# SSD stage of a hybrid decoder step: the chunk state updated ahead of skip and gate, and the memory stages' first rows loaded a stage earlier

## The chip, the cores and the metric

One core of one Trainium2 chip runs the whole program. The metric is device time in microseconds (us) of one execution; lower is better. The kernel before was timed three times: 4456.8 us median, 4452.07 to 4466.3.

## What is computed

One inference step of a decoder trunk for a prompt of 1024 tokens and 8 sample tokens, all in float32. What matters here:

- The input projection gives, besides the attention's q, k and v, the columns z, xBC and dt of a Mamba-2 state-space layer (SSD). xBC goes through a causal convolution over 4 tokens and SiLU. The prompt is scanned in 8 chunks of 128 tokens: within a chunk `y_diag = (C B^T * decay) (x dt)`; from the state carried in, `y_off = C state * exp(cs)`; then `state = chunk_decay * state + B^T (x dt decay_to_end)`.
- The chunk's output is `y = (y_diag + y_off + D x) * SiLU(z)` and then RMS normalised. The sum of the first two terms is called `y`, `D x` is the skip, `SiLU(z)` the gate.
- The 8 sample tokens take one recurrent step of the same layer from a stored state.
- `x += concat(rmsnorm(attention), rmsnorm(ssd)) @ w_out`, then `x +=` cross-attention into 256 memory tokens, then `x +=` an expert layer with 128 retrieved experts per token, then a final norm.

## The kernel before, in words

The program is a chain of stages, each a block of five instruction streams (PE, ACT, DVE, POOL, SP) with semaphores of its own; a barrier of all engines ends each (`Stage.__exit__`). The order is: attention of the prompt, attention of the samples, `ssd_prompt`, `ssd_sample_inputs`, `memory_kv_and_sample_step`, `memory_read`, `memory_read_sample`, `expert_mix`. The last one takes about two thirds of the time. Within a stage each engine runs its instructions in the written order, and a wait holds up all that stands behind it on its engine.

**`ssd_prompt`** works in turns. In turn (t, u = t + 1) the engines finish chunk t ("back") and prepare chunk u ("front"). PE: `tokens(t)` (transposes `xs0`, `xs1` at L1054, the B and C products `bc`, and `yo0`, `yo1`, which multiply C by the state, L1093), decays G0 (L1101), the four projections x0, x1, x2, dt of chunk u (L1062), decays G1, transposes of xBC, the scan, projection z0, the state products `grown` (L1130), projection z1, `summed`. DVE: `tokens`, `scaled` (writes the rows of chunk t - 1), `begin_y`, `middle(u)` (evacuates x0 and x2, L1383), `decays`, half of the convolution taps (L995, L999), `rates`, `finish(t)` (L1425), `summed(u)`. ACT: `tokens(t)` (copies `xs0`, `xs1` out of PSUM, L1195), `middle`, `decays`, `channels`, `convolved`, `gated(t)` (L1243: waits for `y_gated`, squares `y`), `gates(u)` (L1249: SiLU(z) into `zs`), `summed(u)` (exponentials). POOL does the skip `xskip`, the other half of the taps and the norm's factor.

PSUM banks are shared by name in a fixed order (`back_fills`): bank 4 is used by `xs0`, `yo1` and `yd1`, bank 5 by `xs1`, G0, G2 and `st0`, bank 6 by `bc`, G1, G3 and `st1`, bank 7 by `yo0` and `yd0`. A fill waits until the engine that reads the bank's last content has freed it. `st0` and `st1` are the two halves of the chunk's state products, `yd0` and `yd1` those of `y_diag`. `finish(t)` holds the edit: it adds `yd0` and `yd1` to `y` (L1429), adds the skip (L1432), multiplies by the gate (L1434), signals `y_gated`, and then multiplies the state (L1438), adds `st0` and `st1` (L1443) and signals `state_ready`, for which PE's `yo0` of the next chunk waits.

**`memory_kv_and_sample_step`** does two things at once. PE and ACT turn the 256 memory tokens into keys `mk` and values `mv` (`w_mk`, `w_mv`), and PE transposes the keys for DVE to copy into `mkT`. DVE makes the samples' recurrent step over the 4 MB state, which lies in the buffer of `w_out`. SP loads all inputs, stores the new state, then loads the first half of `w_out` (L1689), stores the step's result `y_pairs` (L1692), loads the second half of `w_out` (L1693), loads the result back in another layout as `y` (L1695), stores `mk` and `mv`, and stores the normalised `y` as the samples' rows of the scratch tensor `mixed` (L1701). `y` goes through DVE (skip, gate, L1799 and L1801), ACT (square, L1759), POOL (factor) and DVE (scale, L1808).

**`memory_read`** takes the first two tiles of 128 prompt tokens (`READ = 2`) through `w_out`, the norm and the cross-attention. SP loads `mixed` rows, `x`, the gain of the next norm, `w_mq`, `w_mo`; PE transposes the rows (`turn_mixed`, L1914), DVE multiplies by the gain (`mixed_rows`, L2084; it first waits for `gain_in`, L2150), and PE starts the residual (L1931). PE's priming signals (L1999 to L2002) come ahead of the first transposes; SP's first load waits for one of them.

**`memory_read_sample`** does the same for the 8 sample tokens; it loads their `mixed` rows (L2211) and `x` (L2212), and PE starts with transposes (L2240).

Of the kernel before, what the change touches and what calls it, by code (L numbers as in the profile page):

```python
# [32 lines left out]
P = 128  # L33
# [873 lines left out]
def ssd_prompt(nc, io, psum, shared, w_zx):  # L907
# [7 lines left out]
    with Stage(nc) as stage:  # L915
# [428 lines left out]
        def _(dve):  # L1344
# [80 lines left out]
            def finish(t):  # L1425
# [4 lines left out]
                dve.drain()  # L1430
                dve.wait_ge(xskip_ready.sem, xskip_ready.this(t))
                nc.vector.tensor_tensor(y[:], y[:], xskip[:], ALU.add)  # L1432
                dve.drain()
                nc.vector.tensor_tensor(y[:], y[:], zs[:], ALU.mult)  # L1434
                dve.drain()
                dve.sem_inc(y_gated.sem, 1)

# [7 lines left out]
                dve.sem_inc(state_ready.sem, 1)  # L1445

# [183 lines left out]
def memory_kv_and_sample_step(nc, io, psum, shared, mkT, mv, w_out, w_mo, w_out_in):  # L1630
# [9 lines left out]
    with Stage(nc) as stage:  # L1640
# [26 lines left out]
        def _(sp):  # L1667
# [14 lines left out]
            sp.dma_start(w_mv[:], io["w_mv"].rearrange("(b p) n -> p b n", p=P)).then_inc(wv_in, 16)  # L1682
            sp.wait_ge(state_ready, 1)
# [50 lines left out]
        def _(act):  # L1734
# [36 lines left out]
        def _(dve):  # L1771
# [29 lines left out]
            nc.vector.tensor_tensor(y[:], y[:], gates[:], ALU.mult).then_inc(gated, 1)  # L1801
            for m in range(MT):
# [4 lines left out]
            dve.wait_ge(yrstd_ready, 1)  # L1807
            nc.vector.tensor_scalar(y[:], y[:], yrstd[:], None, ALU.mult).then_inc(out_ready, 1)  # L1808
# [1651 lines left out]
```

## Time and profile before

| what | value |
|---|---|
| median of the runs | 4456.8 us (4452.07 to 4466.3) |
| the profiled execution's own time | 4453.82 us |
| its span, first to last instruction | 4452.0 us |
| mean granted TensorE clock | 0.939 |
| PE busy | 3833.0 us (86%) |
| DVE busy | 2495.7 us (56%) |
| ACT busy | 1309.2 us (29%) |
| POOL busy | 1356.9 us (30%) |

The page gives busy times by engine, then by groups of instructions (line, engine, operation, tile). Times in a timeline are microseconds from the span's start. "PEld" is PE's weight load, "SPq" and "DVEq" the sequencers of SP and DVE. The text in brackets at the end of a row is how long the engine had been idle, and what released it. The granted clock is given as a share of full speed: 1.00 is 2.4 GHz, 0.50 is 1.2 GHz. The SSD stage of the prompt lies at about 490 to 1028 us, the samples' inputs until 1074, the memory keys until 1168, the read until 1343, the sample read until about 1500 and the experts after it.

### The profile page before, as it was taken

Reading aid. Unit: us, or ns where it says so; the run is one execution under the profiler, and the core shown is the slowest. Engines: PE = TensorE matmul, PEld = TensorE weight load, DVE = VectorE, ACT = ScalarE, POOL = GpSimd, SP = SyncE. Lnnn points to the kernel's source line nnn. Section 1 sums busy time; section 2 is a strip of 40 time slices with the busy share of each in tenths; the row PEclk is TensorE's granted clock in tenths of the full one; section 3 lists DMA queues with packets and bytes.
Section 4 is the critical chain, followed back from the end, with each engine's and each line's share of the span. In section 5 each row is a group of like instructions: output and inputs, shape, how many; then the busy total and the mean of one; then the engine's idle time right before and its main releaser. Section 6 shows DMA issues by size and latency. Waiting matters only on the chain.

```text
span 4452.0 us, 41910 instructions
## 1 busy us (share of the span) xinstructions
PE 3833.0 (86%) x11597; PEld 1973.0 (44%) x11597; DVE 2495.7 (56%) x5472; ACT 1309.2 (29%) x3879; POOL 1356.9 (30%) x1243
## 2 busy tenths in 40 slices
PE   8998789887788799998889999889999888877876
PEld 4555254552362445543445554345554344433332
DVE  2333255663312477654577754587755468766664
ACT  2333032331011133342233342323324233333332
POOL 0000033330000133443433434433344343333442
PEclk9996799998897899999999999999999999999999
DMA  6001000004604599999999999999999999999997
GB/s 211 29 28 39 28 15 19 19 9 142 245 10 166 208 418 418 419 418 421 420 403 405 418 420 420 421 399 406 411 420 414 421 419 402 418 418 397 419 420 297
DMA packets 227230, 1316.62 MB, mean 296 GB/s; under 512 B 27224, under 2 KB 43517, under 8 KB 93344
## 3 DMA queue, kind: packets, MB, share of 16 engines
q0 software_dynamic: 148608, 1082.20, 58.8%
q1 hardware_dynamic: 77272, 232.15, 13.9%
q8 instruction: 79, 1.29, 0.1%
q14 instruction: 119, 0.97, 0.1%
q10 hardware_dynamic: 1152, 0.00, 0.0%
HBM read 1283.65 MB, written 32.68 MB: 296 GB/s over the span
## 4 chain that ended last, share of the span: by engine, by line
DMA 27%; PE 25%; DVE 8%; issue 3%; ACT 3%; DVEq 1%; ACTq 0%; POOL 0%; POOLq 0%
DMA ex_ring<-in_expert_uv,ex_idx 26%; PE psum L2752 16%; DVE ex_ring L3137 4%; PE psum L2781 4%; PE psum L2730 3%; ACT ex_diag L2933 1%; PE psum L2800 1%; ACT ex_weight L2928 0%; PE psum L2825 0%; DMA ex_ring<-in_expert_uv,ex_idxT 0%; PE psum L2842 0%; POOL ex_ring L2672 0%; DMA pair_p<-scratch_mixed 0%; DVE ex_best_at L3063 0%; ACT ex_dots L2924 0%
## 5 line engine op out<-in xcount | busy, mean ns | idle before, releaser
L2752 PE MATMUL psum<-ex_ring,ex_diag 128*128 128x512 f32 x4096 | 1920.2, 613 | 332.4 <-ACT ex_diag L2933 308.4
L3137 DVE CUSTOM_DVE_ANT_0 ex_ring<-ex_ring,ex_x_rows 128x1024 f32<-128x1024 f32 x1024 | 1250.5, 1226 | 827.6 <-DMA ex_ring<-in_expert_uv,ex_idx 755.6
L2672 POOL DMA_INDIRECT ex_ring<-in_expert_uv,ex_idx x1024 | 1139.8, 1113 | 1751.4 <-PE psum L2752 1544.1
L2752 PEld LDWEIGHTS psum<-ex_ring,ex_diag 128*128 128x128 f32 x4096 | 771.7, 195 | 1304.9 <-issue 851.6
L2924 ACT ACTIVATE ex_dots<-ex_dots 128x2 f32<-128x2 f32 x512 | 104.1, 203 | 1792.1 <-DVEq L3140 1791.6
L2933 ACT ACTIVATE ex_diag<-ident,ex_weight 128x128 f32<-128x128 f32 x1024 | 355.0, 393 | 36.9 <-issue 1.7
L1062 PE MATMUL psum<-w_zx,ssd_hT 128*128 128x512 f32 (+1 forms) x768 | 294.2, 539 | 21.8 <-DMA ssd_hT<-scratch_hT 21.1
L2730 PE MATMUL psum<-ex_xT,ex_chunk 128*128 128x256 f32 (+1 forms) x1280 | 277.9, 361 | 4.2 <-ACT ex_sub L2909 2.9
L2730 PEld LDWEIGHTS psum<-ex_xT,ex_chunk 128*128 128x128 f32 x1280 | 230.2, 192 | 98.3 <-issue 77.3
L2928 ACT ACTIVATE ex_weight<-ex_gates,ex_dots 128x1 f32<-128x1 f32 x1024 | 245.7, 287 | 36.2 <-issue 1.1
L1062 PEld LDWEIGHTS psum<-w_zx,ssd_hT 128*128 128x128 f32 x768 | 136.9, 192 | 175.1 <-issue 153.1
L320 PE MATMUL psum<-w_qkv,att_hT 128*128 128x512 f32 x384 | 186.6, 633 | 10.6 <-DMA w_qkv<-in_w_in 4.3
L2781 PE MATMUL psum<-ex_chunk,pair_turned_rows 128*128 128x512 f32 x384 | 180.5, 592 | 0.0
L320 PEld LDWEIGHTS psum<-w_qkv,att_hT 128*128 128x128 f32 x384 | 73.5, 201 | 101.4 <-issue 94.1
L615 DVE TENSOR_TENSOR att_turned<-psum,bias 128x512 f32<-128x512 f32 (+1 forms) x64 | 41.8, 658 | 99.8 <-PE psum L347 98.8
L2781 PEld LDWEIGHTS psum<-ex_chunk,pair_turned_rows 128*128 128x128 f32 x384 | 71.1, 190 | 59.9 <-issue 57.4
L536 POOL TENSOR_TENSOR att_ms<-att_ms,att_part 128x1 f32<-128x1 f32 x8 | 1.5, 189 | 303.3 <-ACTq L446 303.3
L2800 PE MATMUL psum<-pair_turned_rows,ex_chunk 128*128 128x256 f32 x384 | 90.7, 379 | 0.0
L2842 PE MATMUL psum<-ex_chunk,pair_turned_rows 128*128 128x512 f32 x192 | 90.2, 592 | 0.0
L1383 DVE TENSOR_SCALAR ssd_xbc<-psum,ssd_rstd 128x512 f32<-128x512 f32 x16 | 12.0, 750 | 131.0 <-PE psum L1062 131.0
L2800 PEld LDWEIGHTS psum<-pair_turned_rows,ex_chunk 128*128 128x128 f32 x384 | 72.8, 190 | 28.2 <-issue 20.6
L3137 DVE DVE_READ_ACCUMULATOR2_ANT ex_dots<- 128x1 f32 x1024 | 83.8, 82 | 0.0
(455 smaller groups left out, 3707.6 us busy)
## 6 DMA issues: line engine op xcount, KB each, us to landing
ex_chunk<-in_route_wq SPq DMA_DIRECT2D x80, 512.0 KB, 7.9
ex_chunk<-in_w_out SPq DMA_DIRECT2D x48, 512.0 KB, 9.1
ex_ring<-in_expert_uv,ex_idx POOLq DMA_INDIRECT x1024, 20.5
ex_chunk<-in_read_wq SPq DMA_DIRECT2D x24, 512.0 KB, 8.0
ex_chunk<-in_w_mo SPq DMA_DIRECT2D x24, 512.0 KB, 7.9
w_zx<-in_w_in SPq DMA_DIRECT2D x1, 10304.0 KB, 35.8
w_out<-in_w_out SPq DMA_DIRECT2D x2, 4096.0 KB
w_out<-in_cache_mem_k SPq DMA_DIRECT2D x8, 1024.0 KB, 13.5
```

What stands on the lines that cost most here:

```text
L320: ins = nc.tensor.matmul(out[:], hT[:, b, :], w_qkv[:, b, c * BANK:(c + 1) * BANK], start=(b == 0), stop=(b == DB - 1))
L1062: ins = nc.tensor.matmul(out[:, 0:n], hT[:, b, :], w_zx[:, b, col:col + n], start=(b == 0), stop=(b == DB - 1))
L2672: nc.gpsimd.indirect_dma_start(out=ring[:, n % RING, :], out_offset=None, in_=io["expert_uv"], in_offset=bass.IndirectOffsetOnAxis(ap=idx[ ...
L2730: ins = nc.tensor.matmul(psum[6 + k % 2][:, 0:n], w[:, b, :], xT[:, b, 0:n], start=(b == 0), stop=(b == DB - 1))
L2752: ins = nc.tensor.matmul(psum[c][:], diag[:, q % 3, s, :], ring[:, n % RING, D + c * BANK:D + (c + 1) * BANK], start=(n % SLOTS == 0), sto ...
L2781: ins = nc.tensor.matmul(psum[2 + 2 * a + c][:], mT[:, b, a * P:(a + 1) * P], w[:, c * BANK:(c + 1) * BANK], start=(b == 0), stop=(b == 2 ...
L2800: ins = nc.tensor.matmul(psum[2 + d % 4][:, 0:N], w[:, b, :], hT[:, b, :], start=(b == 0), stop=(b == DB - 1), skip_group_check=True)
L2842: ins = nc.tensor.matmul(psum[2 + 2 * a + c][:], oT[:, b, a * P:(a + 1) * P], w[:, c * BANK:(c + 1) * BANK], start=(b == 0), stop=(b == DB ...
L2924: nc.scalar.activation(dots[:, q % 8, :], dots[:, q % 8, :], ACT.Gelu)
L2928: nc.scalar.activation(weight[:, q % 2, s:s + 1], gates[:, g % 2, a, at:at + 1], ACT.Copy, scale=dots[:, q % 8, s:s + 1])
L2933: ins = nc.scalar.activation(diag[:, q % 3, s, :], ident[:], ACT.Copy, scale=weight[:, q % 2, s:s + 1])
L3137: nc.vector.tensor_tensor_reduce(ring[:, n % RING, 0:D], ring[:, n % RING, 0:D], x_rows[:, tile % 3, :], 1.0, 0.0, ALU.mult, ALU.add, dots ...
```

## The change

In `finish`, the state update is put ahead of skip and gate:

```diff
                     nc.vector.tensor_tensor(y[:, cols], y[:, cols], src[:], ALU.add).then_inc(free, 1)
-                dve.drain()
-                dve.wait_ge(xskip_ready.sem, xskip_ready.this(t))
-                nc.vector.tensor_tensor(y[:], y[:], xskip[:], ALU.add)
-                dve.drain()
-                nc.vector.tensor_tensor(y[:], y[:], zs[:], ALU.mult)
-                dve.drain()
-                dve.sem_inc(y_gated.sem, 1)
-
                 nc.vector.tensor_tensor(by_head(state[:]), by_head(state[:]), per_head(esums[:, 1, :]), ALU.mult)
...
                 dve.drain()
                 dve.sem_inc(state_ready.sem, 1)
+                dve.wait_ge(xskip_ready.sem, xskip_ready.this(t))
+                nc.vector.tensor_tensor(y[:], y[:], xskip[:], ALU.add)
+                dve.drain()
+                nc.vector.tensor_tensor(y[:], y[:], zs[:], ALU.mult)
+                dve.drain()
+                dve.sem_inc(y_gated.sem, 1)
```

In `memory_kv_and_sample_step`, SP loads the first 128 rows of `mixed` and the samples' `x` behind `w_mv`; `y` is loaded ahead of the second half of `w_out`, and stored ahead of `mv`; ACT squares `y` ahead of the second tile of `mv`; DVE scales `y` ahead of the copies into `mkT`:

```diff
             sp.dma_start(w_mv[:], io["w_mv"].rearrange("(b p) n -> p b n", p=P)).then_inc(wv_in, 16)
+            sp.dma_start(mixed_rows[:], io["mixed"][0:P, :]).then_inc(rows_in, 16)
+            sp.dma_start(own_x[:], io["x_sample"]).then_inc(own_in, 16)
...
-            sp.dma_start(w_out[:, DB:2 * DB, :], w_out_rows[:, DB:2 * DB, :]).then_inc(w_out_in, 16)
             sp.wait_ge(pairs_stored, 16)
             sp.dma_start(y[:], io["rows3"]).then_inc(y_in, 16)
+            sp.dma_start(w_out[:, DB:2 * DB, :], w_out_rows[:, DB:2 * DB, :]).then_inc(w_out_in, 16)
             sp.wait_ge(k_ready, MT)
             sp.dma_start(io["p_mem_k"].rearrange("(m p) n -> p m n", p=P), mk[:]).then_inc(stored, 16)
+            sp.wait_ge(out_ready, 1)
+            sp.dma_start(io["mixed"][SEQ:TOKENS, D:2 * D], y[:]).then_inc(out_stored, 16)
             sp.wait_ge(v_ready, MT)
             sp.dma_start(io["p_mem_v"].rearrange("(m p) n -> p m n", p=P), mv[:]).then_inc(stored, 16)
-            sp.wait_ge(out_ready, 1)
-            sp.dma_start(io["mixed"][SEQ:TOKENS, D:2 * D], y[:]).then_inc(out_stored, 16)
...
             for m in range(MT):
+                if m == 1:
+                    act.wait_ge(gated, 1)
+                    nc.scalar.activation(junk[0:DEC, :], y[:], ACT.Square, accum_out=yms[:]).then_inc(yms_ready, 1)
                 act.wait_ge(projected, 4 + 2 * m + 2)
...
-            act.wait_ge(gated, 1)
-            nc.scalar.activation(junk[0:DEC, :], y[:], ACT.Square, accum_out=yms[:]).then_inc(yms_ready, 1)
...
             nc.vector.tensor_tensor(y[:], y[:], gates[:], ALU.mult).then_inc(gated, 1)
+            dve.wait_ge(yrstd_ready, 1)
+            nc.vector.tensor_scalar(y[:], y[:], yrstd[:], None, ALU.mult).then_inc(out_ready, 1)
             for m in range(MT):
...
             dve.drain()
-            dve.wait_ge(yrstd_ready, 1)
-            nc.vector.tensor_scalar(y[:], y[:], yrstd[:], None, ALU.mult).then_inc(out_ready, 1)
```

In `memory_read`, the buffer `mixed` is now the one filled a stage before. SP's order is `x`, `w_mq`, second `mixed` rows, `w_mo`, gain, second `x`; once the second turn's rows have been transposed, it loads the samples' `mixed` rows into the same buffer. DVE's wait for the gain moves to its first use:

```diff
-            load_mixed(0)
             load_x(0)
-            sp.dma_start(gain_ffn[:], io["norm_ffn_w"].broadcast_to([P, D])).then_inc(gain_in, 16)
             sp.dma_start(w_mq[:], io["w_mq"].rearrange("(b p) n -> p b n", p=P)).then_inc(w_mq_in, 16)
+            sp.sem_inc(mixed_in.sem, 16)
             load_mixed(1)
             sp.dma_start(w_mo[:], io["w_mo"].rearrange("(b p) n -> p b n", p=P)).then_inc(w_mo_in, 16)
+            sp.dma_start(gain_ffn[:], io["norm_ffn_w"].broadcast_to([P, D])).then_inc(gain_in, 16)
             load_x(1)
+            sp.wait_ge(mixed_turned.sem, mixed_turned.last(READ))
+            sp.dma_start(mixed[0:DEC, :], io["mixed"][SEQ:TOKENS, :]).then_inc(own_in, 16)
...
             def turn_mixed(u):
-                pe.wait_ge(mixed_in.sem, mixed_in.this(u))
+                if u:
+                    pe.wait_ge(mixed_in.sem, mixed_in.this(u))
+                else:
+                    pe.wait_ge(rows_in, 16)
...
             def ffn_rows(t):
 
+                if t == 0:
+                    dve.wait_ge(gain_in, 16)
...
-            dve.wait_ge(gain_in, 16)
             mixed_rows(0)
```

In `memory_read_sample`, the loads of the rows and of `x` go; `x` lies in `x1`, to which the projection is added:

```diff
-            sp.dma_start(mixed[:], io["mixed"][SEQ:TOKENS, :]).then_inc(loaded, 16)
-            sp.dma_start(x[:], io["x_sample"]).then_inc(loaded, 16)
...
-            pe.wait_ge(loaded, 32)
+            pe.wait_ge(own_in, 32)
...
-            dve.wait_ge(loaded, 32)
+            dve.wait_ge(own_in, 32)
...
-                ins = nc.vector.tensor_tensor(x1[:, cols], psum[1 + c][0:DEC, :], x[:, cols], ALU.add)
+                ins = nc.vector.tensor_tensor(x1[:, cols], psum[1 + c][0:DEC, :], x1[:, cols], ALU.add)
```

The buffer `mixed` and the semaphores `rows_in` and `own_in` are made in `program`, ahead of the memory stages.

## Rows read from the trace of the kernel before

**Rows 1.** Waits, 560 to 1040 us: waiter <- releaser: us in all, times, longest.

```profile
PE psum L1054 <- DVE ssd_state L1443: 22.3, 7, 3.9
...
PEld psum L1093 <- ACT ssd_xs L1185: 8.9, 8, 1.3
```

**Rows 2.** Timeline, end of one chunk: start, duration, engine, line, operation, [idle before <- releaser].

```profile
744.54 1.28 DVE L1429 TENSOR_TENSOR ssd_y<-ssd_y,psum 128x512 f32<-128x512 f32 x2 [0.19 <-issue]
...
745.92 1.23 DVE L1432 TENSOR_TENSOR ssd_y<-ssd_y,ssd_xskip 128x1024 f32<-128x1024 f32 x1
...
748.50 1.06 ACT L1245 ACTIVATE ssd_junk<-ssd_y 128x1024 f32<-128x1024 f32 x1 [3.15 <-DVEq L1435]
...
749.86 1.28 DVE L1443 TENSOR_TENSOR ssd_state<-ssd_state,psum 128x512 f32<-128x512 f32 x2
...
750.60 1.11 PE L1054 MATMUL psum<-ident,ssd_cv 128*128 128x128 f32 x4 [2.34 <-DVE ssd_state L1443]
...
753.70 1.08 ACT L1185 ACTIVATE ssd_xs<-psum 128x512 f32<-128x512 f32 x2 [0.98 <-issue]
...
756.66 1.15 PE L1101 MATMUL psum<-tri,ssd_decay 128*128 128x128 f32 x8 [0.24 <-issue]
```

**Rows 3.** Timeline, DVE in the middle of the same chunk.

```profile
717.38 0.75 DVE L1383 TENSOR_SCALAR ssd_xbc<-psum,ssd_rstd 128x512 f32<-128x512 f32 x1 [12.98 <-PE psum L1062]
...
724.12 2.04 DVE L995 TENSOR_TENSOR ssd_cv<-ssd_xbcT,conv 128x768 f32<-128x768 f32 x1
```

**Rows 4.** Windows: stretch, length, busy us of PE, PEld, DVE, ACT, POOL, granted clock, DMA.

```profile
754.00:756.00 2.00, 2.00 (x3) 0.50 (x2) 1.15 (x1) 0.79 (x2) 1.10 (x1) 0.50 0.03 0
```

**Rows 5.** Timeline, the end of the next chunk.

```profile
809.58 1.06 ACT L1245 ACTIVATE ssd_junk<-ssd_y 128x1024 f32<-128x1024 f32 x1 [3.15 <-DVEq L1435]
...
815.44 1.12 PE L1093 MATMUL psum<-ssd_state,ssd_cv 128*128 128x512 f32 x2 [0.24 <-ACT ssd_xs L1185]
...
816.80 1.15 PE L1101 MATMUL psum<-tri,ssd_decay 128*128 128x128 f32 x8 [0.24 <-issue]
```

**Rows 6.** Timeline, the last chunk's end.

```profile
1015.16 3.75 PE L1130 MATMUL psum<-ssd_xend,ssd_bm 128*128 128x512 f32 x4 [0.38 <-issue]
...
1018.37 1.06 ACT L1245 ACTIVATE ssd_junk<-ssd_y 128x1024 f32<-128x1024 f32 x1 [6.39 <-DVEq L1435]
```

**Rows 7.** Timeline, the tail of memory_kv_and_sample_step.

```profile
1148.98 0.28 SPq L1695 DMA_DIRECT2D step_y<-scratch_rows  x1
...
1149.74 0.47 SPq L1699 DMA_DIRECT2D out_p_mem_v<-mv  x1
1159.40 1.21 DVE L1799 TENSOR_TENSOR step_y<-step_y,step_xs 8x1024 f32<-8x1024 f32 x1 [16.51 <-DMA step_y<-scratch_rows]
...
1165.14 0.30 SPq L1701 DMA_DIRECT2D scratch_mixed<-step_y  x1
```

**Rows 8.** DMA issues, 1060 to 1550 us: line, queue, count, KB, us to landing.

```profile
out_p_mem_v<-mv SPq DMA_DIRECT2D x1, 1024.0 KB, 14.8
```

**Rows 9.** Timeline, the start of memory_read_sample.

```profile
1343.49 0.30 SPq L2211 DMA_DIRECT2D rs_mixed<-scratch_mixed  x1
...
1346.90 1.87 PE L2240 MATMUL psum<-ident,rs_mixed 8*128 8x8 f32 x16 [12.32 <-DMA rs_x<-in_x_sample]
```

**Rows 10.** Timeline, the start of memory_read.

```profile
1169.34 0.36 SPq L1872 DMA_DIRECT2D read_mixed<-scratch_mixed  x1
...
1174.22 1.97 PE L1914 MATMUL psum<-ident,read_mixed 128*128 128x128 f32 x8 [24.57 <-DMA read_mixed<-scratch_mixed]
...
1178.34 1.97 PE L1914 MATMUL psum<-ident,read_mixed 128*128 128x128 f32 x8 [2.16 <-DVE read_mT L2084]
...
1181.23 30.34 PE L1931 MATMUL psum<-w_out,read_mT 128*128 128x512 f32 x64 [0.92 <-DVEq L2091]
```

**Rows 11.** Windows around PE's transposes of the memory tokens (L1712).

```profile
1080.80:1084.37 3.57, 3.56 (x16) 3.27 (x16) 2.07 (x3) 3.41 (x5) 0.89 (x2) 0.53 1.01 403
1084.37:1087.78 3.41, 0.00 (x1) 0.00 (x0) 0.69 (x1) 0.16 (x1) 0.00 (x0) 0.97 1.03 419
```

More of the change, by code:

```diff
@@ L1627, in _, with memory_kv_and_sample_step @@
             nc.vector.tensor_tensor(dt[:], raw[:], neg[:], ALU.add).then_inc(dt_ready, 1)
-def memory_kv_and_sample_step(nc, io, psum, shared, mkT, mv, w_out, w_mo, w_out_in):
+def memory_kv_and_sample_step(nc, io, psum, shared, mkT, mv, w_out, w_mo, own_x, mixed_rows, w_out_in, rows_in, own_in):
     ident, gain = shared["ident"], shared["gain_mem"]
@@ L1806, in _, with memory_read @@
             dve.drain()
-            dve.wait_ge(yrstd_ready, 1)
-            nc.vector.tensor_scalar(y[:], y[:], yrstd[:], None, ALU.mult).then_inc(out_ready, 1)
-def memory_read(nc, io, psum, shared, w_out, w_mq, w_mo, mkT, mv, w_out_in):
+def memory_read(nc, io, psum, shared, w_out, w_mq, w_mo, mkT, mv, mixed, w_out_in, rows_in, own_in):
     ident = shared["ident"]
@@ L1820, in memory_read @@
         sb, sem, event = stage.buffer, stage.semaphore, stage.event
-        mixed = sb("read_mixed", [P, 2 * D])
         x = sb("read_x", [P, D])
@@ L2154, in _, with memory_read_sample @@
             ffn_rows(READ - 1)
-def memory_read_sample(nc, io, psum, shared, w_out, w_mq, w_mo, x1):
+def memory_read_sample(nc, io, psum, shared, w_out, w_mq, w_mo, x1, mixed, own_in):
     ident = shared["ident"]
@@ L2166, in memory_read_sample @@
         sb, sem = stage.buffer, stage.semaphore
-        mixed, x, junk, q = sb("rs_mixed", [DEC, 2 * D]), sb("rs_x", [DEC, D]), sb("rs_junk", [DEC, D]), sb("rs_q", [DEC, D])
+        junk, q = sb("rs_junk", [DEC, D]), sb("rs_q", [DEC, D])
         mT, hT = sb("rs_mT", [P, 2 * DB, DEC]), sb("rs_hT", [P, DB, DEC])
@@ L2185, in memory_read_sample @@
         v = [places[b % VP] for b in range(DEC)]
-        loaded, turned, mT_ready, summed, x1_ready = (sem("rs_" + n) for n in ("loaded", "turned", "mT_ready", "summed", "x1_ready"))
+        turned, mT_ready, summed, x1_ready = (sem("rs_" + n) for n in ("turned", "mT_ready", "summed", "x1_ready"))
         x1_turned, hT_ready, ms_ready, rstd_ready, projected, q_ready = (
@@ L3398, in program @@
             ssd_sample_inputs(nc, io, psum, shared, w_zx)
-        w_out_in = nc.alloc_semaphore("w_out_in")
+        w_out_in, rows_in, own_in = (nc.alloc_semaphore(n) for n in ("w_out_in", "mixed_rows_in", "own_rows_in"))
         mkT, mv = sb("mkT", [P, DB, N_MEM]), sb("mv", [P, N_MEM // P, D])
@@ L3405, in program @@
             w_mo = memory.enter_context(nc.sbuf_tensor("w_mo", [P, DB, D], F32))
-            memory_kv_and_sample_step(nc, io, psum, shared, mkT, mv, w_out, w_mo, w_out_in)
+            mixed = memory.enter_context(nc.sbuf_tensor("read_mixed", [P, 2 * D], F32))
+            memory_kv_and_sample_step(nc, io, psum, shared, mkT, mv, w_out, w_mo, x1, mixed, w_out_in, rows_in, own_in)
             w_mq = memory.enter_context(nc.sbuf_tensor("w_mq", [P, DB, D], F32))
-            memory_read(nc, io, psum, shared, w_out, w_mq, w_mo, mkT, mv, w_out_in)
-            memory_read_sample(nc, io, psum, shared, w_out, w_mq, w_mo, x1)
+            memory_read(nc, io, psum, shared, w_out, w_mq, w_mo, mkT, mv, mixed, w_out_in, rows_in, own_in)
+            memory_read_sample(nc, io, psum, shared, w_out, w_mq, w_mo, x1, mixed[0:DEC, :], own_in)
         expert_mix(nc, io, psum, shared, mkT, mv)
```

## The prediction

> **What bounds the kernel now.** I read four views: the waits over the SSD stage, the timeline of one chunk's end, the timeline of the memory stages, and the DMA issues. The long expert stage after them is not edited and begins behind a barrier, so what the early stages gain or lose arrives at the end unchanged.
>
> In the waits, PE has one wait that the first edit aims at: its transposes at L1054 (`xs1`, whose PSUM bank the state update frees) stand 22.3 us in all, seven times, for the state adds at L1443. Below it stands a smaller one: the matmuls of `yo1` at L1093 wait for ACT's copy of `xs0` (L1185) [rows 1]. The timeline shows both in one chunk end [rows 2]. DVE adds `y` until 745.82, adds the skip at 745.92, gates, and ACT squares at 748.50; the state adds end at 749.86 + 1.28 = 751.14, and PE resumes at 750.60, in the middle of them. But PE does not run on freely: ACT copies `xs0` only at 753.70, and the decays of L1101 (G0), which precede the next projection, start at 756.66. In the code ACT is strictly ordered: convolved, gated (waits `y_gated`), gates, summed, then the next chunk's tokens. From `y_gated` to the `xs` copies ACT needs 753.70 - 748.50 = 5.2 us. `yo1` shares bank 4 with `xs0`, G0 shares bank 5 with `xs1`, so both need those copies.
>
> Is that a closed loop? DVE's evacuation of `x2` waits 12.98 us for PE's projection, and its taps begin at 724.12 and run until the finish at 744.54 [rows 3, 2]. So PE's projections lead to DVE's taps, to the finish, to `y_gated`, to ACT's copies, and back to PE. A delay of `y_gated` delays the whole chunk.
>
> **SSD: the moved state update.** Removed is one drain; moved are the state multiply, its drain, two adds and their drain, from behind `y_gated` to ahead of it. Before, the state part ends 751.14 - 748.50 = 2.64 us after `y_gated` [rows 2]. With the saved drain (about 0.1, the gap 745.82 to 745.92) and the overlap of two signals I take 2.5 us per chunk by which `y_gated` is later; ends 2.4 and 2.6. `xskip` and the state fills are long there (the `grown` matmuls precede projection z1), so nothing new is waited for. What is queued behind the wait on ACT: square, two gates, the exponentials and the `xs` copies, hence PE's `yo1`, G0 and DVE's `xdt`.
>
> PE's own gain is real but goes nowhere: `xs1`, `bc` and `yo0`, which now run from 750.60 to about 754 at the slow clock, would start 2.6 us sooner and be done near 751. PE would then wait for ACT until 753.70 + 0.55 (one of the two copies) + 2.5, about 756.8: one idle stretch of nearly 6 us in place of 2.34.
>
> The clock is the second price. At this boundary the granted clock is 0.50, the 1.2 GHz level, at 754 to 756 [rows 4], and from ACT's square to G0 pass 756.66 - 748.50 = 8.16 us. At another boundary PE is nearer the 2.4 GHz level and it is 816.80 - 809.58 = 7.22 us; there `yo1` takes 1.12 us and is plainly released by ACT [rows 5]. The seven lie between, so about 0.5 us per chunk is paid already. After an idle of 6 us I expect PE to restart at the low level, so that `yo1`, G0 and the first projections run slowly. Here, after an idle of 2.34 us, the low level went on from PE's restart at 750.60 to about G0 at 756.66, 6.1 us [rows 2]. Half of that, 3.0, is the most that I charge, less the 0.5 already paid; with a little for slower drains, +2.9. The other end is -0.5, if PE comes back at full clock. I take +1.7, nearer the high end, because the nearest row is a shorter idle that already cost clock.
>
> Seven boundaries: 7 x (2.5 + 1.7) = 29.4 us. The eighth finish has no next chunk. There PE's state matmuls run from 1015.16 to 1018.91 and ACT squares at 1018.37 [rows 6]; afterwards the second state add waits for 1018.91, ends near 1019.6, and skip and gate (2.6) bring `y_gated` to about 1022.3: +3.9, which the scaled rows, the state copies into `y` and the last store follow. SSD together +33.3, ends 7 x (2.4 - 0.5) + 3.5 = +16.8 and 7 x (2.6 + 2.9) + 4.5 = +43.
>
> **Memory keys and sample step.** The 1 MB of first mixed rows and the 32 KB of `x_sample` go onto SP's queue behind `w_mv`, ahead of the state's store; SP stands idle there waiting for DVE, and the queue drains before that store. Cost 0; if the cover were gone, 1 MB. At the tail, `y`'s load is issued at 1148.98 and used at 1159.40, held up behind the second half of `w_out`; its result is stored at 1165.14 [rows 7]. With the load ahead of that half, `y` is there about 3 us after issue, some 7 us earlier, and ACT's square (now ahead of the second `mv` copy), DVE's scaling (now ahead of four mkT copies) and the out store follow. But the same bytes still go: 4 MB of `w_out` now start only after 1149.3, when the queue has run dry, and the stores of `mem_k` and `mem_v` come behind. `mem_v` was issued at 1149.74 and landed 14.8 us later, 1164.5 [rows 7, 8]; a dry queue costs up to the 3.4 us that the sample's loads need from issue to use (1346.90 less 1343.49, [rows 9]), which puts `mem_v` at 1167 to 1168, about where the stage ended. Also the added waits: ACT's wait for `gated` holds back the second `mv` copy and so the `mem_v` store; it and SP's `out_ready` wait end near 1157, ahead of the queue's drain. I take 0, ends -2.5 and +2.5.
>
> **Memory read.** PE's first transposes start at 1174.22 on a load issued at 1169.34, the second pair at 1178.34, and the residual at 1181.23 [rows 10]. Afterwards the rows are there, and DVE no longer waits for the gain. SP's first load had to wait for PE's priming, so PE can start near 1169.4; first pair 1.97 and from the second pair to the residual 1181.23 - 1178.34 = 2.89, with a tenth between: residual at 1174.4, 6.8 us earlier; I take 6.6, ends 5.0 and 9.5. `w_mq` and `w_mo` are needed only after the residual's 30.34 us; the gain load, moved behind `w_mo`, is hidden by the whole first tile. The new SP wait for the second turn holds only the store of `x2`, much later.
>
> Would the clock rise sooner? In the stage before, 16 transposes (3.56 us) at 0.53 were followed by 0.97 [rows 11]: transposes alone did bring the clock up, so part of the high end 9.5 is real. The Trainium skill says otherwise: "TensorE: Matmul & The Clock Gate", Part 4, has transposes not counting as busy; by it this stage gives 6.6 and no more, while the row allows up to the whole 9.5. The trace disagrees with that sentence. I keep 6.6, since here the transposes come in two pairs with a gap.
>
> **Sample read.** The two loads go; PE starts at the barrier, near SP's first load, 1343.49, and a signal, in place of 1346.90 [rows 9]: -3.2, ends -2.5 and -3.5.
>
> **Sum.** +33.3 + 0 - 6.6 - 3.2 = +23.5 us. The profiled execution's own time is 4453.8, so 4477.3; the median of the runs shown is 3.0 higher, so 4480. Ends: +16.8 - 15.5 = +1.3 and +43 - 5 = +38, or 4458 and 4495. A difference of 0.3%, 13.4 us, is about what a measurement of this kernel can tell.
>
> **Rivals.** *PE's wait is the bound (faster).* If the state update is what PE's chunk waits for, 22.3 us go, the last finish costs 3.9, the memory stages give 9.8: 4456.8 - 28.2, about 4429. It decides if ACT's `xs` copies would not be late, that is if `y_gated` had more than 2.5 us of slack. For it: it is PE's largest wait in the stage. Against: ACT's square itself starts 0.05 us after DVE's gate ends, and PE is released by ACT [rows 1, 5]. 6%. The Trainium skill, "Perfetto Trace Analysis", Optimization Strategy, has one look for the gaps of the bound engine and make what blocks them start sooner; read on the largest gap alone, it gives this rival. The trace shows the next blocker right behind.
> *The clock costs nothing more (same).* 17.5 + 3.9 in SSD, memory at its best -12: +9.4, 4466, within 0.3%. For it: the present idle already lowers the clock at several boundaries. 17%.
> *The clock stays low longer (slower still).* +43 - 5: 4495. 12%.
> My forecast has 65%. The range 4460 to 4494 holds it, most of the second rival and much of the third. Faster 0.08 (the first rival and a little of the second's tail), same 0.16, slower 0.76.
>
> **What would show it.** Right: PE's wait on L1443 gone; the wait of L1093 on ACT's `xs` grown to about 6 us, seven times; chunk period about 4 us longer; the granted clock low at G0; ACT's square about 2.5 us later after the adds; residual about 6 us after SP's first load of the read stage instead of 12; sample PE at its stage's start. Wrong: a chunk period unchanged or shorter, or `yo1` released by something other than ACT.

## The result, and the profile after

| | before | after |
|---|---|---|
| median of 7 runs, us | 4455.2 (4448.4 to 4466.3) | 4478.0 (4474.9 to 4481.9) |
| profiled span, us | 4452.0 | 4473.1 |
| mean granted clock | 0.939 | 0.940 |

The ratio is 1.0048, interval 1.0039 to 1.0057: slower by 17 to 25 us. The forecast was 4480.

Where the 21.1 us of the two spans lie is read from the timelines, from the start of one stage's first operation to that of the next:

| stretch | before, us | after, us | difference | predicted |
|---|---|---|---|---|
| start to G0 of the first SSD chunk | 574.27 | 571.93 | -2.3 | not edited |
| SSD, to the sample inputs' first load | 454.35 | 486.53 | +32.2 | +33.3 |
| sample inputs | 45.86 | 45.08 | -0.8 | not edited |
| memory keys and sample step | 94.86 | 96.86 | +2.0 | 0 |
| memory read | 174.15 | 167.26 | -6.9 | -6.6 |
| sample read, to the experts' first load (before: at 1485.2) | 141.73 | 140.45 | -1.3 | -3.2 |
| expert stage to the end | 2966.8 | 2965.0 | -1.8 | not edited |

The unedited stretches differ by up to 2.3 us; a difference of that size in one row is not evidence of anything.

**SSD.** The waits of the changed kernel over 560 to 1070 us (waiter <- releaser: us in all, times, longest):

```profile
ACT ssd_junk L1245 <- DVEq L1442: 49.8, 8, 10.1
PEld psum L1093 <- ACT ssd_xs L1185: 48.2, 8, 6.9
PE psum L1093 <- ACT ssd_xs L1185: 36.2, 7, 5.3
...
PE psum L1054 <- DVE ssd_state L1435: 7.0, 7, 1.2
```

The wait that the edit aimed at fell from 22.3 us to 7.0 [rows 1]. A new one of 36.2 us stands in its place: `yo1` on ACT's copy of `xs0`. (The 8.9 us of [rows 1] are of the weight loads, PEld; their row is now 48.2.) The sum of PE's waits rose. The timeline of the same chunk end shows why (start, duration, engine, line, operation, idle before and releaser):

```profile
750.71 1.28 DVE L1429 TENSOR_TENSOR ssd_y<-ssd_y,psum 128x512 f32<-128x512 f32 x2 [0.19 <-issue]
751.91 1.22 DVE L1430 TENSOR_TENSOR ssd_state<-ssd_state,ssd_esums 128x1024 f32<-128x1024 f32 x1
...
753.20 1.29 DVE L1435 TENSOR_TENSOR ssd_state<-ssd_state,psum 128x512 f32<-128x512 f32 x2
...
753.94 0.80 PE L1054 MATMUL psum<-ident,ssd_cv 128*128 128x128 f32 x4 [0.97 <-DVE ssd_state L1435]
...
757.21 1.06 ACT L1245 ACTIVATE ssd_junk<-ssd_y 128x1024 f32<-128x1024 f32 x1 [5.69 <-DVEq L1442]
...
762.41 1.08 ACT L1185 ACTIVATE ssd_xs<-psum 128x512 f32<-128x512 f32 x2 [0.98 <-issue]
...
763.06 2.07 PE L1093 MATMUL psum<-ssd_state,ssd_cv 128*128 128x512 f32 x2 [5.27 <-ACT ssd_xs L1185]
...
765.37 2.07 PE L1101 MATMUL psum<-tri,ssd_decay 128*128 128x128 f32 x8 [0.24 <-issue]
```

From the start of DVE's `y` adds to ACT's square it is 757.21 - 750.71 = 6.50 us, where it was 748.50 - 744.54 = 3.96 [rows 2]: 2.54 later. ACT's own 5.2 us from the square to the `xs` copies did not change (762.41 - 757.21). PE resumed its transposes 1 us after it stopped in place of 2.34, ran `yo0`, and then stood 5.27 us in front of `yo1`.

The windows of the same stretch (length, busy us of PE, PEld, DVE, ACT, POOL, granted clock, DMA) show the second price:

```profile
757.00:763.00 6.00, 0.79 (x1) 0.00 (x0) 0.51 (x3) 4.62 (x9) 0.98 (x3) 0.78 0.00 0
763.00:765.00 2.00, 1.94 (x2) 0.50 (x2) 1.24 (x2) 0.49 (x2) 1.40 (x1) 0.50 0.03 0
765.00:767.00 2.00, 1.76 (x8) 1.64 (x8) 2.00 (x3) 0.00 (x0) 1.54 (x1) 0.50 0.00 0
767.00:769.00 2.00, 2.00 (x7) 1.06 (x6) 1.51 (x3) 0.00 (x0) 0.00 (x0) 0.76 0.00 0
769.00:771.00 2.00, 2.00 (x6) 0.85 (x5) 1.16 (x2) 0.00 (x0) 0.00 (x0) 1.00 0.65 262
```

After the idle of 5.27 us PE comes back at 0.50, the 1.2 GHz level, and the clock is at 1.00 again only about 5 us later, within 767 to 769. The idle is not where it first fell: `yo0` already ran at 0.50 (754.4 to 757.7), then the clock stood at 1.00 while PE was idle (757.8 to 761.1) and was at 0.50 again from 761.2, ahead of `yo1`. `yo1` takes 2.07 us where the next chunk end of before had 1.12, and G0 takes 2.07 where it took 1.15 [rows 5].

ACT's eight squares start at 627.32, 692.31, and so on to 1016.67 and 1048.35; before, at 627.13, 687.56, to 990.87 and 1018.37. The six periods between the first seven are 389.35 us, 64.89 each, against 363.74, 60.62 each: +4.27, where the prediction had 2.5 + 1.7 = 4.2. The last finish:

```profile
1041.47 3.43 PE L1130 MATMUL psum<-ssd_xend,ssd_bm 128*128 128x512 f32 x4 [0.38 <-issue]
...
1044.94 0.69 DVE L1435 TENSOR_TENSOR ssd_state<-ssd_state,psum 128x512 f32<-128x512 f32 x1 [0.70 <-PE psum L1130]
...
1048.35 1.06 ACT L1245 ACTIVATE ssd_junk<-ssd_y 128x1024 f32<-128x1024 f32 x1 [10.06 <-DVEq L1442]
```

The second state add waits for PE's state matmuls, as predicted. From their start to the square it is 6.88 us; it was 3.21 [rows 6]: +3.7, predicted +3.9.

**Keys stage.** The timeline of its tail, and the start of the read stage:

```profile
1179.93 0.29 SPq L1694 DMA_DIRECT2D step_y<-scratch_rows  x1
1180.27 0.38 SPq L1695 DMA_DIRECT2D w_out<-in_w_out  x1
...
1181.79 1.21 DVE L1800 TENSOR_TENSOR step_y<-step_y,step_xs 8x1024 f32<-8x1024 f32 x1 [9.51 <-DMA step_y<-scratch_rows]
...
1187.23 0.31 SPq L1699 DMA_DIRECT2D scratch_mixed<-step_y  x1
1187.58 0.37 SPq L1701 DMA_DIRECT2D out_p_mem_v<-mv  x1
...
1200.40 0.36 SPq L1876 DMA_DIRECT2D read_x<-in_x_prompt  x1
1201.92 3.51 PE L1916 MATMUL psum<-ident,read_mixed 128*128 128x128 f32 x16 [23.82 <-issue]
1206.50 27.70 PE L1936 MATMUL psum<-w_out,read_mT 128*128 128x512 f32 x64 [1.07 <-DVEq L2096]
```

`y` is used 1.9 us after its load is issued, where that took 1159.40 - 1148.98 = 10.4 [rows 7]. The stage is no shorter, for it now ends on the store of `mem_v`. The DMA issues give it (line, queue, count, KB, us to landing):

```profile
out_p_mem_v<-mv SPq DMA_DIRECT2D x1, 1024.0 KB, 11.5
```

Issued at 1187.58, it lands at 1199.1, and the read stage's first load goes out at 1200.40. The store has 4 MB of `w_out` and 1 MB of `mem_k` ahead of it; both were issued only once `rows3` had made its round trip, and in that time the queue ran dry:

```profile
1178.50:1181.50 3.00, 0.00 (x0) 0.00 (x0) 0.00 (x0) 0.00 (x0) 0.00 (x0) 0.91 0.38 109
```

That is a window of 3 us in which the DMA engines moved 109 GB/s; the windows of 3 us on both sides moved 410 and 317. Whether this gap costs the stage its 2.0 us is settled with `fed_queue`, at the end of the experiments: it does not.

**Memory read.** The residual starts 1206.50 - 1200.40 = 6.1 us after the stage's first load, where it was 1181.23 - 1169.34 = 11.9 [rows 10]: 5.8 sooner. It also takes 27.70 us in place of 30.34. The windows of its start, of the changed kernel:

```profile
1201.90:1205.40 3.50, 3.47 (x16) 2.82 (x16) 1.76 (x3) 0.00 (x0) 0.00 (x0) 0.57 0.96 348
1205.40:1206.50 1.10, 0.03 (x1) 0.03 (x1) 0.91 (x2) 0.00 (x0) 0.00 (x0) 1.00 0.98 372
```

All 16 transposes now run in one piece, and the clock stands at 1.00 before the first matmul of the residual. Before, the residual began at 0.50:

```profile
1181.20:1185.00 3.80, 3.77 (x5) 1.73 (x6) 0.00 (x0) 0.00 (x0) 0.00 (x0) 0.50 1.02 413
1185.00:1187.00 2.00, 2.00 (x4) 0.73 (x4) 0.00 (x0) 0.00 (x0) 0.00 (x0) 0.62 1.05 418
```

The 0.62 of the second window puts the rise at 1186.5, so the first 5.3 us of the residual ran at half speed, which is the 2.6 us of its length. So 5.8 + 2.6 = 8.4 us are gained by the residual's end, and the rest of the stage gives 1.5 back.

**Sample read.** PE starts with the stage:

```profile
1367.66 0.30 SPq L2217 DMA_DIRECT2D rs_gain_ffn<-in_norm_ffn_w  x1
1367.71 1.84 PE L2244 MATMUL psum<-ident,read_mixed 8*128 8x8 f32 x16 [9.03 <-PEq L127]
```

That is 0.05 us after SP's first load in place of 3.41 [rows 9], a gain of 3.4. At the stage's end 1.3 of it is left: the loads of `k` come 2.9 us sooner, but DVE then waits 15.8 us for the next projection, where it waited 14.1. That projection takes longer:

```profile
1402.79 15.60 PE L2250 MATMUL psum<-w_mq,rs_hT 128*8 128x512 f32 x32 [0.32 <-DVE rs_hT L2338]
```

Before, it took 13.90 us, all at 1.00. Here the granted clock was 0.50 from 1402.86 to 1406.20, and once more in this stage from 1484.8 to 1488.1. Of the kernels below, which all have this stage, `mem_only`, `both` and `filler` take 13.90 us for the projection and 138.2, 138.0 and 138.2 us for the stage: 3.5 to 3.8 less than before. `w_out_back` and `fed_queue` take 15.60, and 140.4 and 140.5 like this kernel. So the edit gains about 3.5 us here, and the two low stretches of this execution hid about 2 of them.

### The profile page after: what moved, and what is told of

Same layout as the page of the kernel before. It is cut to its first block, busy times and chain, and to the rows that moved or that the text cites. A ratio compares the mean times of both kernels' runs of the same rounds, so it can differ in the third digit from the quotient of the medians.

```text
span 4473.1 us, 41903 instructions
## 1 busy us (share of the span) xinstructions
PE 3836.9 (86%) x11597; PEld 1971.7 (44%) x11597; DVE 2495.2 (56%) x5472; ACT 1308.6 (29%) x3879; POOL 1365.8 (31%) x1243
## 4 chain that ended last, share of the span: by engine, by line
DMA 27%; PE 24%; DVE 7%; issue 3%; ACT 3%; DVEq 1%; ACTq 0%; POOL 0%; POOLq 0%
DMA ex_ring<-in_expert_uv,ex_idx 26%; PE psum L2756 16%; DVE ex_ring L3141 4%; PE psum L2785 3%; PE psum L2734 3%; ACT ex_diag L2937 1%; PE psum L2804 1%; ACT ex_weight L2932 0%; PE psum L2829 0%; DMA ex_ring<-in_expert_uv,ex_idxT 0%; PE psum L2846 0%; POOL ex_ring L2676 0%; DMA pair_p<-scratch_mixed 0%; DVE ex_best_at L3067 0%; DVE ex_top_at L3036 0%
## 5 line engine op out<-in xcount | busy, mean ns | idle before, releaser
L2932 ACT ACTIVATE ex_weight<-ex_gates,ex_dots 128x1 f32<-128x1 f32 x1024 | 245.7, 287 | 36.2 <-issue 1.1
L1062 PEld LDWEIGHTS psum<-w_zx,ssd_hT 128*128 128x128 f32 x768 | 138.0, 193 | 175.4 <-issue 153.7
L320 PE MATMUL psum<-w_qkv,att_hT 128*128 128x512 f32 x384 | 187.9, 637 | 11.2 <-DMA w_qkv<-in_w_in 4.3
L320 PEld LDWEIGHTS psum<-w_qkv,att_hT 128*128 128x128 f32 x384 | 73.9, 202 | 102.5 <-issue 94.9
```

Source lines behind the costliest of these rows:

```text
L320: ins = nc.tensor.matmul(out[:], hT[:, b, :], w_qkv[:, b, c * BANK:(c + 1) * BANK], start=(b == 0), stop=(b == DB - 1))
L1062: ins = nc.tensor.matmul(out[:, 0:n], hT[:, b, :], w_zx[:, b, col:col + n], start=(b == 0), stop=(b == DB - 1))
L2932: nc.scalar.activation(weight[:, q % 2, s:s + 1], gates[:, g % 2, a, at:at + 1], ACT.Copy, scale=dots[:, q % 8, s:s + 1])
```

## The experiments

The theory: a chunk's start on PE is released by two signals that lie close together. One is the state adds (bank 5, hence `xs1`); the other is ACT's `xs` copies, which stand behind the gated `y` in ACT's order (banks 4 and 5, hence `yo1` and G0). The edit speeds the first and delays the second, and PE comes out of the longer idle at a low clock. The rival of that: the loss is in PE's or DVE's own work, or in the memory stages. Ratios below are each against the kernel before, timed beside it on the same chip (median 4457.7 for the first four, 4457.1 for the others).

**The two halves of the change alone.** `ssd_only` is the kernel before with the diff of `finish`, and nothing of the memory stages:

```diff
-                dve.drain()
-                dve.wait_ge(xskip_ready.sem, xskip_ready.this(t))
...
                 nc.vector.tensor_tensor(by_head(state[:]), by_head(state[:]), per_head(esums[:, 1, :]), ALU.mult)
...
                 dve.sem_inc(state_ready.sem, 1)
+                dve.wait_ge(xskip_ready.sem, xskip_ready.this(t))
+                nc.vector.tensor_tensor(y[:], y[:], xskip[:], ALU.add)
...
+                dve.sem_inc(y_gated.sem, 1)
```

> The kernel before with the state update ahead of skip and gate, and none of the memory edits. My theory: ACT's copies of xs, which wait for the gated y, close the loop; y is gated 2.5 us later in each of seven chunks, the lower clock after PE's longer idle adds about 1.7, and the last chunk's end 3 to 4: +32 us, 4487 (4480 to 4493). The rival, PE's wait for the state adds is the bound and 22.3 us of it go: about 4437.

Measured: 4489.2, ratio 1.0075 (1.0058 to 1.0092). From the first G0 to the sample inputs' first load it takes 1065.86 - 578.45 = 487.4 us against 454.35: +33.1, where the prediction's sum for SSD was +33.3. Its waits over 560 to 1070 us:

```profile
PE psum L1093 <- ACT ssd_xs L1185: 37.9, 7, 6.8
...
PE psum L1054 <- DVE ssd_state L1435: 7.1, 7, 1.1
```

`mem_only` is the changed kernel with the old `finish`:

```diff
+                dve.drain()
+                dve.wait_ge(xskip_ready.sem, xskip_ready.this(t))
+                nc.vector.tensor_tensor(y[:], y[:], xskip[:], ALU.add)
...
+                dve.sem_inc(y_gated.sem, 1)
                 nc.vector.tensor_tensor(by_head(state[:]), by_head(state[:]), per_head(esums[:, 1, :]), ALU.mult)
...
                 dve.sem_inc(state_ready.sem, 1)
-                dve.wait_ge(xskip_ready.sem, xskip_ready.this(t))
...
-                dve.sem_inc(y_gated.sem, 1)
```

> The kernel before with the memory edits and the old order in DVE's finish. My theory from the prediction: the keys stage unchanged, the read 6.6 us and the sample read 3.2 us shorter: -9.8, 4445. From the trace of the changed kernel: keys stage 2 us longer, read 6.9 and sample read 1.3 shorter: -6, 4449. The rival, that the slow time came from the memory stages: above 4460.

Measured: 4444.9, ratio 0.9974 (0.9963 to 0.9985). Its PE waits in SSD are those of before (22.4 us on the state adds; 8.9 of the weight loads on the copies). So the loss is all in SSD, and the memory edits are a gain of 7 to 16 us by themselves. The two halves sum to +31.5 - 12.8 = +18.7; the whole change measured +22.8 in its own runs.

**The other blocker alone, and both.** If ACT's `xs` copies are the second releaser, moving them ahead of `gated` takes that signal off the gated `y`. `act_only` does this to the kernel before, in ACT's `turn`:

```diff
                     load_rstd(u)
-                if back:
-                    tokens(t)
                 if front:
                     middle(u)
...
                     convolved(u)
+                    tokens(u)
                 if back:
                     gated(t)
```

> The kernel before, with ACT copying the next chunk's xs ahead of squaring the gated y, so that nothing of PE's chunk start waits for the gated y any more. If ACT's copies alone set the chunk before (so that the state adds were fully hidden): about 2.5 us a chunk go, 4437. If the two blockers were near a tie, as the timelines with yo1 only 0.24 us behind yo0 suggest: -0.2 to -1 a chunk, 4451 (4446 to 4456). If ACT's order has no part in it: 4455.

Measured: 4454.6, ratio 1.0002 (0.999 to 1.0013). The time excludes 4437, the case of ACT's copies alone, but it cannot tell a near tie (4451) from no part at all (4455). The trace tells more. ACT's copies no longer hold `yo1`, but PE still stands for the state adds; its waits over 560 to 1040 us:

```profile
PE psum L1054 <- DVE ssd_state L1442: 20.8, 7, 4.0
PEld psum L1093 <- issue: 6.9, 16, 0.5
```

A chunk takes (985.69 - 624.66) / 6 = 60.17 us, 0.45 less than before. `both` is the same edit in the changed kernel:

```diff
-                if back:
-                    tokens(t)
...
                     convolved(u)
+                    tokens(u)
                 if back:
                     gated(t)
```

> The changed kernel with ACT copying the next chunk's xs ahead of squaring the gated y. If the gated y blocks PE through ACT's order alone, the moved state update now pays: PE goes from xs0 to the projections without a long wait, about 7 us a chunk less than in the changed kernel (4.2 given back and some 3 of the old wait), 4428 (4418 to 4438), well below both kernels. If something else of the moved update made the chunk longer (DVE's order, the clock by itself), it stays above 4465.

Measured: 4425.2, ratio 0.9937 (0.9921 to 0.9954). A chunk takes (973.76 - 629.79) / 6 = 57.33 us, 7.6 less than in the changed kernel and 3.3 less than before. Its waits over 560 to 1030 us, and one chunk end:

```profile
PE psum L1062 <- ACT ssd_zs L1185: 5.2, 4, 1.6
...
PE psum L1054 <- DVE ssd_state L1434: 4.0, 4, 1.0
```

```profile
742.10 1.08 ACT L1185 ACTIVATE ssd_xs<-psum 128x512 f32<-128x512 f32 x2 [3.19 <-PE psum L1054]
...
744.60 1.06 ACT L1245 ACTIVATE ssd_junk<-ssd_y 128x1024 f32<-128x1024 f32 x1 [1.42 <-DVEq L1441]
...
745.12 1.15 PE L1101 MATMUL psum<-tri,ssd_decay 128*128 128x128 f32 x8 [0.24 <-issue]
...
747.30 15.29 PE L1062 MATMUL psum<-w_zx,ssd_hT 128*128 128x512 f32 x35 [1.03 <-ACT ssd_zs L1185]
```

```profile
744.00:748.00 4.00, 2.73 (x13) 1.48 (x12) 2.89 (x6) 3.15 (x5) 1.84 (x3) 1.00 0.00 0
```

At this end G0 starts 0.52 us after ACT's square instead of 8.16 (0.14 to 1.84 us at the seven ends), with the clock at 1.00, and the next blocker is a third one: the bank of `z1`, which ACT's gates free behind their wait for the gated `y`. The four kernels make a table:

| | state update behind the gate | state update first |
|---|---|---|
| ACT's copies behind `gated` | 4457.7 (before) | 4478.0 (after); 4489.2 without the memory edits |
| ACT's copies first | 4454.6 | 4425.2, with the memory edits |

Each edit alone gives nothing or a loss. Together, and with the memory edits' 12.8 us set aside, they give 4457.7 - 12.8 - 4425.2 = 19.7 us by the medians. No kernel with both edits and without the memory edits was run. The trace of `both` gives less: its SSD takes 439.3 us against 454.35, so 15.0.

**The clock.** `filler` adds matmuls to the changed kernel, one behind the transposes of `xs0` and four between `yo0` and `yo1`, into front bank 0. Their results are read by nobody; they only keep PE busy where it stood idle.

```diff
+                def fill_time(n):
+                    pe.wait_ge(front_fills.free[0], front_fills.at("x2", t + 1))
+                    for b in range(n):
+                        nc.tensor.matmul(psum[0][:], ident[:], w_zx[:, b, 0:BANK], start=True, stop=True)
...
                 for g in range(SSD_G):
+                    if g:
+                        fill_time(4)
                     out, full = begin(f"yo{g}", t)
```

> The changed kernel with five extra matmuls a chunk (one behind xs0, four between yo0 and yo1), whose results nobody reads, in the time in which PE waits for ACT. If the lower clock after that idle is a price of its own (G0 2.07 us in place of 1.15, the projections behind it 1.2 us longer): the granted clock stays up, -1.2 to -2 a chunk, 4468 (4463 to 4473). If the chunk is only later by the gated y: 4478.

Measured: 4471.9, ratio 1.0033 (1.0018 to 1.0047). The time is as expected, but the clock did not stay up as a whole: it held at the start of two of the six chunks only, and the mean chunk is 1.16 us shorter, just under the expected 1.2 to 2. The windows around G0 at one such chunk end, and at one where it fell:

```profile
768.00:770.00 2.00, 1.75 (x11) 1.29 (x11) 1.80 (x4) 0.00 (x0) 2.00 (x1) 1.00 0.00 0
...
704.00:705.00 1.00, 0.88 (x5) 0.88 (x6) 0.80 (x2) 0.00 (x0) 1.00 (x1) 0.66 0.00 0
705.00:707.00 2.00, 2.00 (x7) 1.48 (x7) 2.00 (x3) 0.00 (x0) 1.24 (x1) 0.50 0.00 0
```

The two chunks with the clock held take 823.92 - 761.25 = 62.67 and 1015.11 - 952.42 = 62.69 us; the other four 64.15 to 64.35; the changed kernel's 64.89. This prices the clock: 64.89 - 62.68 = 2.2 us per chunk. Without it the chunk is still 62.68 - 60.62 = 2.06 longer than before. That is the 2.54 of the later `y` less the half microsecond of clock that the kernel before already paid. PE's idle in front of `yo1` was 3.34 us at four of the six ends: at two of these the clock held, at two it fell within G0. At the other two ends it was 2.14 and 2.17 us, and the clock fell within `yo1`. So the length of that idle does not decide it; what does stays open.

**Half of the move.** `half` is the kernel before with the state multiply alone put ahead of skip and gate:

```diff
+                nc.vector.tensor_tensor(by_head(state[:]), by_head(state[:]), per_head(esums[:, 1, :]), ALU.mult)
                 dve.drain()
                 dve.wait_ge(xskip_ready.sem, xskip_ready.this(t))
...
-                nc.vector.tensor_tensor(by_head(state[:]), by_head(state[:]), per_head(esums[:, 1, :]), ALU.mult)
-                dve.drain()
```

> The kernel before with the state's multiply alone moved ahead of skip and gate; the two state adds stay behind. The gated y is then 1.2 us later in each chunk, in place of 2.5, and the state is ready when it was. If the gated y sets the chunk: +1.2 a chunk and 0 to 0.6 for the clock, seven times, and up to 1.2 at the end: 4469 (4465 to 4473). If the state adds set it: 4457.

Measured: 4468.3, ratio 1.0024 (1.0015 to 1.0033). The time is as expected, but its place is not. The square comes 754.47 - 749.39 = 5.08 us after the `y` adds, 1.12 later than before. Yet five of the six chunks take 61.26 to 61.28, only 0.65 more than before. One of their ends:

```profile
754.47 1.06 ACT L1245 ACTIVATE ssd_junk<-ssd_y 128x1024 f32<-128x1024 f32 x1 [4.27 <-DVEq L1436]
...
760.33 1.13 PE L1093 MATMUL psum<-ssd_state,ssd_cv 128*128 128x512 f32 x2 [0.95 <-ACT ssd_xs L1185]
...
761.69 1.15 PE L1101 MATMUL psum<-tri,ssd_decay 128*128 128x128 f32 x8 [0.24 <-issue]
```

From the square to G0 it is 7.22 us, the full-clock value [rows 5], in each of these five, where before it was 7.75 in the mean: 1.12 - 0.53 = 0.59. A `y` that is 1.12 us later cost no clock there but gave some back. The clock was low there too: PE stood 3.66 us for the state adds, and it was 0.50 over 757 to 759, while `yo0` ran, 0.88 over 759 to 761 and 1.00 over 761 to 763. The low stretch was over when ACT's copies came, where before it went on through `yo1` [rows 4]. The rest lies in the first period (62.99 us against 60.43, with G0 there at a low clock, 1.89 us) and from the seventh square to the last (30.33 against 27.50). From the first G0 to the last square `half` takes 453.65 us against 444.10, +9.6, of the +11.2 of the medians.

**The tail of the keys stage.** `w_out_back` is the changed kernel with the second half of `w_out` issued ahead of `y`'s round trip again, so that the queue does not run dry. It was timed once.

```diff
+            sp.dma_start(w_out[:, DB:2 * DB, :], w_out_rows[:, DB:2 * DB, :]).then_inc(w_out_in, 16)
             sp.wait_ge(pairs_stored, 16)
             sp.dma_start(y[:], io["rows3"]).then_inc(y_in, 16)
-            sp.dma_start(w_out[:, DB:2 * DB, :], w_out_rows[:, DB:2 * DB, :]).then_inc(w_out_in, 16)
```

> The changed kernel with the second half of w_out issued again ahead of the load of y. If the queue that runs dry for 3 us costs the keys stage its 2 us: the values' store lands some 3 us earlier against the stage's start, the queue shows no gap, and the stage is about 95 us in place of 96.9, with y late again (10 us after issue). If the two early loads cost the 2 us: the stage stays at 96.9.

Measured: 4479.6. The keys stage takes 97.9 us, longer than the changed kernel's 96.9, so the expectation failed. The timeline:

```profile
1180.87 0.29 SPq L1695 DMA_DIRECT2D step_y<-scratch_rows  x1
...
1191.36 1.21 DVE L1800 TENSOR_TENSOR step_y<-step_y,step_xs 8x1024 f32<-8x1024 f32 x1 [18.10 <-DMA step_y<-scratch_rows]
...
1196.80 0.30 SPq L1699 DMA_DIRECT2D scratch_mixed<-step_y  x1
1197.15 0.38 SPq L1701 DMA_DIRECT2D out_p_mem_v<-mv  x1
```

`y` is late again (10.5 us from issue to use), and `mem_v`, which in this order stands behind SP's wait for `y`'s result, goes out only at 1197.15. The two edits of the tail belong together: `y` ahead of `w_out` is what makes `y` ahead of `mem_v` harmless.

`fed_queue` is `both` with `mem_k`'s store put into the gap of the round trip:

```diff
+            sp.wait_ge(k_ready, MT)
+            sp.dma_start(io["p_mem_k"].rearrange("(m p) n -> p m n", p=P), mk[:]).then_inc(stored, 16)
             sp.wait_ge(pairs_stored, 16)
             sp.dma_start(y[:], io["rows3"]).then_inc(y_in, 16)
             sp.dma_start(w_out[:, DB:2 * DB, :], w_out_rows[:, DB:2 * DB, :]).then_inc(w_out_in, 16)
-            sp.wait_ge(k_ready, MT)
-            sp.dma_start(io["p_mem_k"].rearrange("(m p) n -> p m n", p=P), mk[:]).then_inc(stored, 16)
```

> The changed kernel with ACT's new order, and with the keys' store issued ahead of SP's wait for the pairs, so that the queue has something to move while y makes its round trip. Against ACT's new order alone (4425): the gap of 3 us is filled, the keys stage 2 to 3 us shorter, 4422. If the stage's end hangs on y and not on the queue: 4425.

Measured: 4428.6, ratio 0.9935 (0.9919 to 0.9951), not to be told from `both` by its time. In the trace the keys stage takes 94.8 us, 1.9 less than that of `both`, and `mem_v` lands 9.3 us after issue. That looks like the 3 us gap, but it is not. The stage's store of the new state, far ahead of the tail, lands after one of two times (DMA issues of before, then of the changed kernel):

```profile
out_s_ssm<-w_out SPq DMA_DIRECT2D x1, 4096.0 KB, 11.8
out_s_ssm<-w_out SPq DMA_DIRECT2D x1, 4096.0 KB, 13.3
```

The first half of `w_out` waits for it, and is issued 61.6 and 63.4 us after the stage's start. Both times come with the memory edits and without them, and the stage's length goes with them:

| the state's store lands after | without the memory edits | with them |
|---|---|---|
| 11.6 to 11.8 us | 94.9 (before), 95.2 (`act_only`), 95.3 (`half`) | 94.4 (`filler`), 94.8 (`fed_queue`) |
| 13.3 us | 97.1 (`ssd_only`) | 96.9 (changed), 97.2 (`mem_only`), 96.6 (`both`), 97.9 (`w_out_back`) |

Within a row the edits change less than 1 us, and `filler`, which has the gap (152 GB/s over 1176 to 1179), is no longer than `fed_queue`, which fills it (371 over 1125 to 1128). So neither the edits nor the dry queue cost the 2.0 us. Why the store's landing differs is not shown.

## Why the prediction was right

**The loop, and the delay of `y`.** Right. The predicted 2.5 us per chunk measured 2.54, and nothing between `y_gated` and G0 absorbed it. `yo1` is released by ACT's copies in all seven boundaries, for 5.2 us on average; the prediction had about 6. The wait for the state adds did not go but fell to 7.0. `act_only` and `both` show the two releasers as such: only with the second gone as well does the first edit pay.

**The clock.** Right in its size: 1.7 predicted beyond what was already paid, 4.27 - 2.54 = 1.7 measured. It lies in two places, in the mean of the six periods: square to G0 is 8.17 us against 7.70, and G0 to the decays of the next group (G1) is 24.54 against 23.30, so 0.5 + 1.2. The two `filler` chunks at full clock confirm it. The reasoning behind it was weaker than its result: 1.7 was a choice between ends of -0.5 and +2.9, so the close match is in part luck. The prediction scaled from the 2.34 us idle of before, and `half` shows that a longer one (3.66 us) need not cost any clock, if the low stretch is over before the second signal comes. (The [rows 2] that it names hold no clock; the trace has 0.50 over 750.60 to 754.00 as well, so that reading stands.)

**The last finish and the SSD sum.** Right: +3.7 against +3.9, and +32.2 against +33.3.

**Keys stage.** Right: 0 predicted. The two mechanisms named, a dry queue and `mem_v` behind `w_out`, are in the trace (3 us at 109 GB/s; landing at 1199.1, which ends the stage), and cost nothing that the traces show. The measured +2.0 is the later landing of the state's store, which `ssd_only` shows without the memory edits. With the store at its earlier time, in `filler`, `mem_v` lands 93.1 us after the stage's start; the prediction's 1167 to 1168 is 92.5 to 93.5.

**Memory read.** -6.6 predicted, -6.9 measured, but of other parts, so the match is luck: the start gave 5.8, since PE began 1.5 us after SP's first load and not at once; the clock gave 2.6, which the prediction had left in its high end because of the two pairs with a gap. There is no gap: all 16 transposes run through. By the rule from the Trainium skill, "TensorE: Matmul & The Clock Gate", Part 4, that transposes do not count as busy, this part would have been nothing; the windows at 0.57 and then 1.00 disagree with it here as [rows 11] did. The gain is not a safe one, though. The same residual took 27.70 us in `mem_only`, `both` and `fed_queue` too, but 30.12 in `filler` and 29.64 in `w_out_back`, where the same 16 transposes ran at 0.50 throughout and the clock rose only within the residual. Over these runs the stage is 4.5 to 8.9 us shorter than before. What decides is not shown, nor whether these transposes, which the trace names MATMUL, are of the kind that the page means.

**Sample read.** Right, though the row of the table does not show it. The start moved by 3.4 us as predicted (3.2). The stage shrank by only 1.3 in this execution, because the clock fell twice in it; in the three kernels where it did not, the stage shrank by 3.5 to 3.8.

**The rivals.** PE's wait as the bound (4429) is excluded by `ssd_only` and by the waits. The clock for nothing (4466) is excluded by 64.89 against 62.68. A clock that stays low longer (4495) did not come: the chunk's 4.27 is that of the forecast.

## What to carry to other kernels

The largest wait of an engine is not what its removal is worth: look for the next signal that the same engine needs, and subtract. Here two releasers lay within a few microseconds, and an edit that took time from one and gave it to the other lost the whole shift on every turn of the loop, while taking both shortened the stage by 15 us. When a chain is put ahead of another on one engine, price the one that is put behind by following its signal through the strictly ordered engines to the loop's start. And before a few microseconds in one stage of one trace are given a cause, compare that stage in the traces of kernels that share its code: here two such differences, of 2 us each, came and went with the execution.

## What the runs showed of the hardware that was not expected

The granted clock after a wait does not follow from the wait's length alone. With 5.3 us of idle ahead of `yo1` it came back at 0.50; with PE filled, it stayed at 1.00 at two ends with 3.34 us of idle, fell to 0.50 within G0 at two others with the same 3.34 us, and fell already within `yo1` at two with 2.14 and 2.17 us. In `half`, whose `y` is 1.12 us later than before, five boundaries had G0 at full speed (1.15 us), and square to G0 took the full-clock 7.22 us, which only one boundary of the kernel before had. The same 16 transposes ahead of the same residual were followed by a clock of 1.00 in four traces and of 0.50 in two. A store of 4 MB landed after 11.6 to 11.8 us in five traces and after 13.3 in the five others, whatever the edits.
